# Building one-hot factors for tile 1's dense expert weights during tile 1's rows, in one layer of a streaming encoder

## The chip, the cores and the metric

One core of a Trainium2 chip runs the kernel. The metric is device time in microseconds (us); three runs of the kernel before took 1350.66, 1354.59 and 1364.85 us, median 1354.59.

## The reference

One layer of an encoder runs over 384 tokens of 1024 floats: 256 new tokens of one stream and 8 streams of 16. Attention in two branches comes first. The part that matters here is the feed-forward part, with 16384 experts of one neuron each:

```
def block(hx):                                   # 128 tokens
    q = (hx @ w_pq).reshape(128, 8, 256)         # 8 heads
    s1, s2 = q[..., :128] @ c1.T, q[..., 128:] @ c2.T
    v1, i1 = top_k(s1, 16);  v2, i2 = top_k(s2, 16)
    cand = v1[..., :, None] + v2[..., None, :]   # 256 pairs
    sv, si = top_k(cand, 16)
    e = (i1 * 128 + i2) at si                    # 16 experts a head
    g = softmax(sv)
    a = gelu(einsum('nhkd,nd->nhk', u[e], hx))
    return einsum('nhk,nhkd->nd', g * a, v[e])
```

So each token has 128 slots, each an expert with two keys (0 to 127) and a weight g * a. The tables u and v have 16384 rows of 1024 floats, 64 MB each.

## The kernel before

There are three tiles of 128 tokens: tiles 0 and 1 (lanes A and B, the new stream) and tile 2 (lane C, the 8 streams, `SAMPLE`). After the opening attention work of lane A, VectorE runs a loop over 512 "rows". Row n, for n below 384, is slot n % 128 of tile n // 128: GpSimd gathers for each of the 128 tokens its row of u into one of six slots of `rows_ring` (L699, 128 x 1024 floats, 512 KB), and VectorE takes the dot product with the token's `h2` (L1680). Rows 384 to 511 are tile 2's rows of v, also gathered, which VectorE multiplies by their weights and adds to `x1` (L1685).

Tiles 0 and 1 do not gather v. Their weights are spread into a dense matrix of token by expert, `dense[t]`, and at the end TensorE multiplies it with the whole of v (L1315): SyncE streams v in 128 blocks of 512 KB through four slots of `ring0`, and each block has two tiles times two halves of products (1024 matmul records in all). This product starts when all 64 groups are in `dense` and lane C's queries are done. The last addition to `x1` (L1696) follows both the product and row 511.

The dense weights are built in groups of four tokens, 32 groups a tile (`dense_weights`, on three engines). First the tile's keys 1, keys 2 and weights are turned (transposed) by TensorE into one PSUM bank (L1288) and copied to `turned` by ScalarE (L923, L924). Then, for each group:

- ScalarE builds the unweighted one-hot factor of key 2: for each token |iota - key2| (L962, four instructions), then relu(1 - that) over the four (L965), into one of two slots of `hot2`.
- VectorE builds the weighted factor of key 1: for each token (iota == key1) * weight (L1667, four instructions), into one of two slots of `hot1`.
- TensorE multiplies the two for each token (L1300, eight matmul records a group) into one of two PSUM banks (`transA`, `accumA`).
- ScalarE copies the bank to `dense` (L947), called "put" below.

The factors wait for the product two groups back, and the product for the put two groups back.

All work beside the rows is laid by step numbers: m is a quarter of the row number, and each engine takes up laid work in the order of its m. On VectorE and GpSimd, which carry the rows, laid work is taken up after every second row, that is at every half step. Tile 1's rows end at m = 64. `DENSE[t]` holds the step of the turning, that of the first group, and the groups per step; `dense_at` makes each group's step from it. Tile 1 has (64.5, 65, 4): turning at 64.5, groups from 65 on, two per pair of rows. The weights of tile 1 (gelu on ScalarE L914, times gate on VectorE L1655) are laid at m = 65 on VectorE. Each engine runs its own instructions strictly in this order, so an instruction that waits holds up all behind it.

Of the kernel before, what the change touches and what calls it, by code (L numbers as in the profile page):

```python
# [14 lines left out]
P = 128  # L15
# [103 lines left out]
def route_at(first, last=3):  # L119
# [25 lines left out]
def build(nc, i, o):  # L145

    with ExitStack() as ctx:  # L147
# [160 lines left out]
        built = [trans[0], accum[0]]  # L308

# [407 lines left out]
        def _(act):  # L717
# [198 lines left out]
            def dense_weights(t):  # L916
# [6 lines left out]
                act.activation(turned[:, 1, :], bank[:, 1, :], ACT.Copy, scale=-1.0).then_inc(S("turned_copied"), 1)  # L923
                act.activation(turned[:, 0::2, :], bank[:, 0::2, :], ACT.Copy).then_inc(S("turned_copied"), 1)  # L924
# [26 lines left out]
                for g in range(TGROUPS):  # L951
                    yield dense_at(t, g)
                    n = t * TGROUPS + g
                    if g == 0:
                        act.wait_ge(S("turned_copied"), 2 * t + 2)
                        act.wait_ge(S("iota_set"), 1)
                        if t == 0:
                            act.wait_ge(to(B, "logits_done"), 2)
                    if n >= 2:
                        act.wait_ge(S("built"), n - 1)  # L960
                    for j, tok in enumerate(tokens_of(t, g)):
                        act.activation(hot2[:, n % 2, j * P:j * P + P], iota[:, :], ACT.Abs,  # L962
                                       bias=turned[:, 1, tok:tok + 1]).then_inc(S("apart"), 1)
                    act.wait_ge(S("apart"), TOKENS * (n + 1))
                    act.activation(hot2[:, n % 2, :], hot2[:, n % 2, :], ACT.Relu, bias=1.0, scale=-1.0).then_inc(  # L965
                        S("hot2_ready"), 1)
                    if g:
                        put(g - 1)
                put(TGROUPS - 1)

            between = [laid(x) for x in (queries(A), softmax_exps(0), softmax_exps(1), groups(GL, LATE_COPY), steps(B),
                                         gate_copies(B), steps(C), gate_copies(C), queries(B), queries(C),
                                         softmax_exps(SAMPLE), gelus(0), dense_weights(0), gelus(1), dense_weights(1),
                                         late_scores(), gelus(SAMPLE))]
# [7 lines left out]
        def _(pe):  # L982
# [295 lines left out]
            def dense_weights(t):  # L1278
# [8 lines left out]
                for n, src in enumerate((keys[:, t, :, 0], keys[:, t, :, 1], dots[:, t, :])):  # L1287
                    ins = pe.transpose(built[0][:, n * P:n * P + P], src, ident[:, :])  # L1288
                ins.then_inc(S("turned"), 1)
                for g in range(TGROUPS):  # L1290
                    yield dense_at(t, g)
                    n = t * TGROUPS + g
                    pe.wait_ge(S("hot2_ready"), n + 1)
                    pe.wait_ge(S("hot1_ready"), n + 1)
                    if g == 1:
                        pe.wait_ge(S("turned_copied"), 2 * t + 2)
                    elif n >= 2:
                        pe.wait_ge(S("dense_put"), n - 1)
                    for j in range(TOKENS):
                        ins = pe.matmul(built[(g + 1) % 2][:, j * P:j * P + P], hot2[:, n % 2, j * P:j * P + P],  # L1300
                                        hot1[t][:, n % 2, j * P:j * P + P], start=True, stop=True)
                    ins.then_inc(S("built"), 1)

            between = [laid(x) for x in (queries(A), project(GL, LATE_PROJ), attention(B), gates(B), finish(B),
                                         attention(C), gates(C), finish(C), queries(B), dense_weights(0), queries(C),
                                         dense_weights(1))]
# [28 lines left out]
        def _(v):  # L1335
# [311 lines left out]
            def weights(t):  # L1647
# [3 lines left out]
                for q in range(parts):  # L1651
                    yield t * STEPS + STEPS // parts * (q + 1) + (2 if t == 0 else 1)
# [4 lines left out]
            def dense_weights(t):  # L1657

                for g in range(TGROUPS):
                    yield dense_at(t, g)  # L1660
                    n = t * TGROUPS + g
                    if g == 0:
                        v.wait_ge(S("turned_copied"), 2 * t + 2)
# [76 lines left out]
```

## Time and profile before

| | |
|---|---|
| median of three runs | 1354.59 us |
| profiled execution, device time | 1354.58 us |
| its span | 1352.8 us |
| TensorE busy | 1095.4 us (81%) |
| VectorE busy | 980.1 us (72%) |
| GpSimd busy | 657.9 us (49%) |
| ScalarE busy | 307.7 us (23%) |
| DMA moved | 460.64 MB, mean 341 GB/s |

The profile is of one execution. Its span is 1.8 us shorter than the device time of the same execution. The shares are averages over stages with different limits, so the rows further down are taken stage by stage: steps 48 to 64, the second build (tile 1's groups, 829 to 907 us), and the product (907 to 1347 us). Times in these rows are us from the start of the span; "idle before" is what an engine stood still just before an instruction, with the releaser behind the arrow.

### The profile page before, as it was taken

The numbers are of one execution on the slowest core, as the hardware profiler recorded it, in microseconds if no ns is written. First come the engines' busy times: TensorE is split into PE (matmuls) and PEld (weight loads), VectorE is DVE, ScalarE is ACT, GpSimd is POOL, SyncE is SP. The second block draws the span as 40 slices with busy tenths as digits, with TensorE's granted clock in tenths as the row PEclk, the third lists the DMA queues.
The fourth block names the chain that finished last, engine by engine and source line by source line (L and its number), as shares of the span: only waits on it lengthen the run. The fifth ranks groups of instructions, "written<-read, shape, count | busy, mean of one in ns | idle before, by whom it ended". The sixth has DMA issues, their size and how long they took to land. (4 is left out here: it accounts for less than half of the span.)

```text
span 1352.8 us, 13110 instructions
## 1 busy us (share of the span) xinstructions
PE 1095.4 (81%) x4321; PEld 732.2 (54%) x4321; DVE 980.1 (72%) x2230; ACT 307.7 (23%) x843; POOL 657.9 (49%) x570
## 2 busy tenths in 40 slices
PE   6888898886686768668566743779999999999998
PEld 3443583342243667325446732666666666666665
DVE  2621069999777799948988998999866566665666
ACT  2132122132311223031444454970000000000000
POOL 2110036557264565446674566566655454444452
PEclk9999899997797879786778865779999999999999
DMA  9985569969899999998997878779999999999998
GB/s 332 329 314 205 206 246 356 338 220 372 336 330 368 391 316 382 381 354 329 336 377 252 303 269 289 237 226 393 409 410 409 409 409 410 410 409 409 410 407 333
DMA packets 167348, 460.64 MB, mean 341 GB/s; under 512 B 14912, under 2 KB 36848, under 8 KB 167024
## 3 DMA queue, kind: packets, MB, share of 16 engines
q0 software_dynamic: 74784, 271.66, 53.7%
q1 hardware_dynamic: 92496, 188.14, 37.5%
q8 instruction: 34, 0.56, 0.2%
q14 instruction: 34, 0.28, 0.1%
HBM read 453.41 MB, written 6.34 MB: 340 GB/s over the span
## 5 line engine op out<-in xcount | busy, mean ns | idle before, releaser
L699 POOL DMA_INDIRECT rows_ring<-in_peer_u,expert x384 | 489.2, 1274 | 393.6 <-DVE dots L1680 293.8
L1680 DVE CUSTOM_DVE_ANT_0 rows_ring<-rows_ring,arena 128x1024 f32<-128x1024 f32 x384 | 458.3, 1223 | 93.1 <-DMA rows_ring<-in_peer_u,expert 89.9
L1315 PE MATMUL wide<-ring,arena 128*128 128x512 f32 x1024 | 440.2, 592 | 0.7 <-issue 0.7
L1315 PEld LDWEIGHTS wide<-ring,arena 128*128 128x128 f32 x1024 | 302.2, 295 | 138.1 <-issue 1.6
L1685 DVE SCALAR_TENSOR_TENSOR x<-rows_ring,dots,x 128x1024 f32<-128x1024 f32 x128 | 164.5, 1285 | 95.3 <-DMA rows_ring<-in_peer_v,expert 94.9
L699 POOL DMA_INDIRECT rows_ring<-in_peer_v,expert x128 | 125.0, 977 | 138.8 <-DVE x L1685 127.2
L962 ACT ACTIVATE hot<-iota,turned 128x128 f32<-128x128 f32 x256 | 81.0, 390 | 0.0
L993 PE MATMUL transB<-ident,arena 128*128 128x128 f32 x165 | 32.8, 329 | 40.3 <-ACT arena L732 15.9
L732 ACT ACTIVATE arena<-transB 128x512 f32<-128x512 f32 (+2 forms) x44 | 24.7, 564 | 126.1 <-PE transB L993 120.6
L993 PEld LDWEIGHTS transB<-ident,arena 128*128 128x128 f32 x165 | 22.1, 165 | 49.1 <-ACT arena L732 19.6
L1300 PE MATMUL accumA<-arena,hot 128*128 128x128 f32 x128 | 24.2, 348 | 29.9 <-ACT hot L965 16.1
L1018 PE MATMUL accumA<-ring,arena 128*128 128x512 f32 (+1 forms) x96 | 40.7, 582 | 7.8 <-DMA ring<-in_w_in 6.6
L1300 PE MATMUL transA<-arena,hot 128*128 128x128 f32 x128 | 25.7, 364 | 25.0 <-ACT hot L965 21.7
L1667 DVE TENSOR_SCALAR arena<-iota,turned 128x128 f32<-128x128 f32 x128 | 35.7, 360 | 8.5 <-PE transA L1300 5.9
L1265 PE MATMUL wide<-arena 128*128 128x128 f32 x320 | 40.8, 293 | 0.8 <-ACT arena L732 0.8
L1265 PEld LDWEIGHTS wide<-arena 128*128 128x128 f32 x320 | 40.3, 210 | 1.1 <-issue 1.1
L965 ACT ACTIVATE hot<-hot 128x512 f32<-128x512 f32 x64 | 40.3, 630 | 2.0
L614 POOL TENSOR_SCALAR ssx<-ssx 128x1 f32<-128x1 f32 x6 | 2.0, 339 | 79.1 <-ACT rows_ring L720 72.0
L1300 PEld LDWEIGHTS accumA<-arena,hot 128*128 128x128 f32 x128 | 21.1, 249 | 34.0 <-ACT hot L965 18.5
L1667 DVE TENSOR_SCALAR gain<-iota,turned 128x128 f32<-128x128 f32 x128 | 35.6, 362 | 5.1 <-PE accumA L1300 3.5
L1018 PE MATMUL accumA<-arena 128*128 128x512 f32 x80 | 35.3, 594 | 2.7 <-ACT accumA L763 1.9
L1300 PEld LDWEIGHTS transA<-arena,hot 128*128 128x128 f32 x128 | 22.1, 259 | 28.6 <-ACT hot L965 24.4
(300 smaller groups left out, 1397.2 us busy)
## 6 DMA issues: line engine op xcount, KB each, us to landing
ring<-in_peer_v SPq DMA_DIRECT2D x128, 512.0 KB, 6.8
arena<-in_w_in SPq DMA_DIRECT2D x15, 2048.0 KB, 16.3
ring<-in_w_in SPq DMA_DIRECT2D x9, 2048.0 KB, 17.2
arena<-in_w_pq SPq DMA_DIRECT2D x7, 2048.0 KB, 13.8
ring<-in_w_pq SPq DMA_DIRECT2D x5, 2048.0 KB, 17.8
arena<-in_w_out SPq DMA_DIRECT2D x4, 2048.0 KB, 10.9
arena<-in_w_br_a SPq DMA_DIRECT2D x3, 2048.0 KB, 10.2
ring<-in_w_br_b SPq DMA_DIRECT2D x3, 2048.0 KB, 12.0
```

Source lines behind the costliest of these rows:

```text
L699: pool.indirect_dma_start(rowbuf[:, n % ROWS, :], None, u_rows if n < U_ROWS else v_rows, index).then_inc(S(f"rows{n % ROWS}"), 16)
L732: ins = act.activation(dst, src, ACT.Copy)
L962: act.activation(hot2[:, n % 2, j * P:j * P + P], iota[:, :], ACT.Abs, bias=turned[:, 1, tok:tok + 1]).then_inc(S("apart"), 1)
L965: act.activation(hot2[:, n % 2, :], hot2[:, n % 2, :], ACT.Relu, bias=1.0, scale=-1.0).then_inc(S("hot2_ready"), 1)
L993: ins = pe.transpose(L.trans[n % count][:, m * P:m * P + P], src, ident[:, :])
L1018: ins = pe.matmul(accum[u % 2][:, 0:GROUPS[g][2]], L.hT[:, c, :], slot_weights(G.name, name)[:, c, :], start=c == 0, stop=c == DC - 1)
L1265: ins = pe.matmul(L.query_banks[k % 2][:, 0:P], slot_weights(L.name, f"pq{q}")[:, c, k * P:k * P + P], L.h2T[:, c, :], start=c == 0, stop= ...
L1300: ins = pe.matmul(built[(g + 1) % 2][:, j * P:j * P + P], hot2[:, n % 2, j * P:j * P + P], hot1[t][:, n % 2, j * P:j * P + P], start=True, ...
L1315: return pe.matmul(wide[:, 2 * t + half, :], dense[t][:, :, b], vblock[:, b % VBLOCKS, half * 512:half * 512 + 512], start=b == 0, stop=b ...
L1667: ins = v.tensor_scalar(hot1[t][:, n % 2, j * P:j * P + P], iota[:, :], turned[:, 0, tok:tok + 1], turned[:, 2, tok:tok + 1], ALU.is_equal ...
L1680: v.tensor_tensor_reduce(row, row, h2[:, t, :], 1.0, 0.0, ALU.mult, ALU.add, dots[:, t, k:k + 1]).then_inc(S("row_used"), 1)
L1685: v.scalar_tensor_tensor(out=x1[:, SAMPLE, :], in0=row, scalar=dots[:, SAMPLE, k:k + 1], in1=x1[:, SAMPLE, :], op0=ALU.mult, op1=ALU.add). ...
```

## The change

Tile 1's factors of key 2 need no weights, only keys, which are known well before the rows end. Seventeen of tile 1's 32 factors are now built by ScalarE between steps 48 and 64, into fifteen stretches of the arena that are part of `dense[1]` or free by then (`AHEAD`; the groups that those stretches belong to, `HELD`, are put last), and the two slots of `hot2`. The keys of tile 1 are turned by TensorE at step 47 into `sumB` and copied at 47.5 into the space of `own` and `new_bias`. The other fifteen factors are built during the second build, one after every second put, each in the place of a factor that was used. In the second build only the weights are turned. The second build is laid earlier and denser: turning at 64, groups from 64.5 at six per step, and the weights at 64 on VectorE.

```diff
-DENSE = [(35, 44, 1.8), (64.5, 65, 4)]
+DENSE = [(35, 44, 1.8), (64, 64.5, 6)]
+AHEAD = [22528, 23040, 23552, 24064, 16384, 16896, 25600, 30208, 18944, 19456, 19968, 20480, 20992, 21504, 22016]
+AHEAD_AT = [48, 49, 50, 51, 52, 53, 54, 55, 56, 57, 58, 61, 61.5, 62, 62.5, 63, 63.5]
+HELD = [(a - BLOCKS * P) // (TOKENS * P) for a in AHEAD]
-         list(range(TGROUPS))]
+         [n for n in range(TGROUPS) if n not in HELD] + HELD]
...
+        ahead = [part(a, TOKENS * P) for a in AHEAD] + [hot2[:, n, :] for n in range(2)]
+        key1_ahead, key2_ahead = new_bias[:, :, :].rearrange("p h k -> p (h k)"), own[:, :]
+        def hot2_of(t, g):
+            return ahead[g % len(ahead)] if t else hot2[:, g % 2, :]
...
# ScalarE, dense_weights
                 for g in range(TGROUPS):
                     yield dense_at(t, g)
+                    if t:
+                        if g:
+                            put(g - 1)
+                        late = len(ahead) + g // 2 - 1
+                        if g and g % 2 == 0 and late < TGROUPS:
+                            act.wait_ge(S("built"), TGROUPS + late - len(ahead) + 1)
+                            one_hots(1, late, key2_ahead)
+                        continue
...
+            def one_hots(t, g, keys2):
+                dst = hot2_of(t, g)
+                for j, tok in enumerate(tokens_of(t, g)):
+                    act.activation(dst[:, j * P:j * P + P], iota[:, :], ACT.Abs, bias=keys2[:, tok:tok + 1]).then_inc(
+                        S(f"apart{t}"), 1)
+                act.wait_ge(S(f"apart{t}"), TOKENS * (g + 1))
+                act.activation(dst, dst, ACT.Relu, bias=1.0, scale=-1.0).then_inc(S(f"hot2_ready{t}"), 1)
+            def one_hots_ahead():
+                yield AHEAD_AT[0] - 0.5
+                act.wait_ge(S("ahead_turned"), 1)
+                act.wait_ge(to(C, "logits_read"), 1)
+                act.activation(key2_ahead, sumB[:, P:2 * P], ACT.Copy, scale=-1.0).then_inc(S("ahead_copied"), 1)
+                act.activation(key1_ahead, sumB[:, 0:P], ACT.Copy).then_inc(S("ahead_copied"), 1)
+                for g in range(len(ahead)):
+                    yield AHEAD_AT[g]
+                    if g == 0:
...
+                    elif g == len(AHEAD):
+                        act.wait_ge(S("built"), TGROUPS)
+                    one_hots(1, g, key2_ahead)
...
# TensorE, dense_weights
-                    ins = pe.transpose(built[0][:, n * P:n * P + P], src, ident[:, :])
+                    if t == 0 or n == 2:
+                        ins = pe.transpose(built[0][:, n * P:n * P + P], src, ident[:, :])
...
+            def keys_ahead():
+                yield AHEAD_AT[0] - 1
+                pe.wait_ge(S("routed"), 8)
+                pe.wait_ge(to(C, "attended"), 2)
+                for n in range(2):
+                    ins = pe.transpose(sumB[:, n * P:n * P + P], keys[:, 1, :, n], ident[:, :])
+                ins.then_inc(S("ahead_turned"), 1)
...
# VectorE, weights and dense_weights
-                    yield t * STEPS + STEPS // parts * (q + 1) + (2 if t == 0 else 1)
+                    yield t * STEPS + STEPS // parts * (q + 1) + (2, 0, 1)[t]
...
+                    keys1 = key1_ahead if t else turned[:, 0, :]
```

VectorE, where the second build begins. The `ISA rows_ring,dots` rows are the dot products (the `ISA dots` rows between them only store their sums), `dots<-dots,gate` makes the weights, `gain<-iota` builds factors of key 1, four instructions a group. Before:

```order
L1680 ISA rows_ring,dots<-rows_ring,arena 128x1024
L1680 ISA dots 128x1
L1655 TENSOR_TENSOR dots<-dots,gate 128x128
L1667 TENSOR_SCALAR gain<-iota,turned 128x128 x4
L1680 ISA rows_ring,dots<-rows_ring,arena 128x1024
L1680 ISA dots 128x1
L1680 ISA rows_ring,dots<-rows_ring,arena 128x1024
L1680 ISA dots 128x1
L1667 TENSOR_SCALAR gain<-iota,turned 128x128 x8
```

Now (line numbers are those of the changed kernel):

```order
L1715 TENSOR_TENSOR dots<-dots,gate 128x128
L1743 ISA rows_ring,dots<-rows_ring,arena 128x1024
L1743 ISA dots 128x1
L1743 ISA rows_ring,dots<-rows_ring,arena 128x1024
L1743 ISA dots 128x1
L1730 TENSOR_SCALAR gain<-iota,new_bias,turned 128x128 x4
L1743 ISA rows_ring,dots<-rows_ring,arena 128x1024
L1743 ISA dots 128x1
L1743 ISA rows_ring,dots<-rows_ring,arena 128x1024
L1743 ISA dots 128x1
L1730 TENSOR_SCALAR gain<-iota,new_bias,turned 128x128 x12
```

The weights moved from behind row 261 to behind row 257, two rows now lie between them and the first group, and three groups instead of two follow each pair of rows; the 32nd group stands behind row 281 instead of row 293.

ScalarE, at the start of the second build, behind the gelu of tile 1 (`dots<-dots`); `hot<-` and, in the change, `arena<-iota,own` are factors of key 2, `arena<-accumA` and `arena<-transA` are puts. Before:

```order
L914 ACTIVATE dots<-dots 128x128
L923 ACTIVATE turned<-transA 128x128
L924 ACTIVATE turned<-transA 128x2x128
L897 ACTIVATE keys<-wide 128x512
L897 ACTIVATE tables<-wide 128x512
L962 ACTIVATE hot<-iota,turned 128x128 x4
L965 ACTIVATE hot<-hot 128x512
L962 ACTIVATE hot<-iota,turned 128x128 x4
L965 ACTIVATE hot<-hot 128x512
L947 ACTIVATE arena<-accumA 128x512
```

Now:

```order
L990 ACTIVATE hot<-iota,own 128x128 x4
L993 ACTIVATE hot<-hot 128x512
L925 ACT_TABLE_LOAD
L925 ACTIVATE dots<-dots 128x128
L935 ACTIVATE turned<-transA 128x128
L908 ACTIVATE keys<-wide 128x512
L908 ACTIVATE tables<-wide 128x512
L961 ACTIVATE arena<-accumA 128x512
L961 ACTIVATE arena<-transA 128x512
L990 ACTIVATE arena<-iota,own 128x128 x4
L993 ACTIVATE arena<-arena 128x512
L961 ACTIVATE arena<-accumA 128x512
```

A factor stood ahead of every put; now one stands behind every second put, and the last factors built ahead stand right ahead of the gelu.

ScalarE, near step 48, where the first factor is built ahead; `arena,ssx<-x` sums the squares for tile 2's row scale. Before:

```order
L947 ACTIVATE arena<-accumA 128x512
L962 ACTIVATE hot<-iota,turned 128x128 x4
L965 ACTIVATE hot<-hot 128x512
L947 ACTIVATE arena<-transA 128x512
L720 ACTIVATE arena,ssx<-x 128x1024
```

Now:

```order
L961 ACTIVATE arena<-accumA 128x512
L990 ACTIVATE arena<-iota,own 128x128 x4
L993 ACTIVATE arena<-arena 128x512
L990 ACTIVATE hot<-iota,turned 128x128 x4
L993 ACTIVATE hot<-hot 128x512
L961 ACTIVATE arena<-transA 128x512
L731 ACTIVATE arena,ssx<-x 128x1024
```

One whole factor now stands between the put and the group ahead of the squares.

## Rows read from the trace of the kernel before

**Rows 1.** Page, part 4: the chain that ended last, its share of the span by line.
```profile
PE wide L1315 33%; ACT hot L962 3%; ACT hot L965 1%; ACT arena L947 1%; PE accumA L1300 0%; DVE x L1696 0%; PE transA L1300 0%; PE transA L1288 0%; ACT keys L897 0%; DVEq L147 0%; ACT tables L897 0%; DVE dots L1655 0%; ACT dots L914 0%; ACT turned L924 0%; ACT turned L923 0%
```

**Rows 2.** Chain that ended last, pieces in order: start us, length us, what.
```profile
830.80 1.15 ACT hot L962 x4
831.97 0.64 ACT hot L965
...
904.36 1.74 PE transA L1300 x8
906.83 440.17 PE wide L1315 x1024
...
1347.07 0.69 DVE x L1696
```

**Rows 3.** Timeline, VectorE: start us, length us, line, operation xcount [idle before <-releaser]; in the second build.
```profile
855.12 1.22 DVE L1680 CUSTOM_DVE_ANT_0 rows_ring<-rows_ring,arena 128x1024 f32<-128x1024 f32 x1
856.26 2.14 DVE L1667 TENSOR_SCALAR gain<-iota,turned 128x128 f32<-128x128 f32 x8
858.32 1.22 DVE L1680 CUSTOM_DVE_ANT_0 rows_ring<-rows_ring,arena 128x1024 f32<-128x1024 f32 x1
```

**Rows 4.** Stretches: busy us (count) of PE, PEld, DVE, ACT, POOL; granted clock, DMA share, GB/s.
```profile
812.00:828.00 16.00, 0.00 (x0) 0.00 (x0) 11.90 (x21) 0.31 (x1) 12.65 (x12) 0.50 0.93 318
829.00:906.80 77.80, 53.89 (x258) 46.12 (x257) 73.39 (x198) 74.83 (x198) 44.34 (x34) 0.71 0.73 236
907.00:1340.00 433.00, 433.00 (x1009) 297.64 (x1010) 289.70 (x438) 6.02 (x9) 222.61 (x212) 1.00 1.02 406
```

**Rows 5.** Groups of VectorE, 906.83 to 1347.1: xcount | busy, mean ns | idle before, releaser.
```profile
L1685 DVE SCALAR_TENSOR_TENSOR x<-rows_ring,dots,x 128x1024 f32<-128x1024 f32 x128 | 164.5, 1285 | 95.3 <-DMA rows_ring<-in_peer_v,expert 94.9
L1680 DVE CUSTOM_DVE_ANT_0 rows_ring<-rows_ring,arena 128x1024 f32<-128x1024 f32 x88 | 106.6, 1225 | 47.2 <-DMA rows_ring<-in_peer_u,expert 46.8
```

**Rows 6.** Timeline, VectorE, 1338 to 1353: the last five rows of v.
```profile
1340.08 6.85 DVE L1685 SCALAR_TENSOR_TENSOR x<-rows_ring,dots,x 128x1024 f32<-128x1024 f32 x5 [0.80 <-DMA rows_ring<-in_peer_v,expert]
```

**Rows 7.** Timeline, VectorE: end of row 257, weights behind row 261, first group.
```profile
821.61 0.08 DVE L1680 DVE_READ_ACCUMULATOR2_ANT dots<- 128x1 f32 x1
...
827.95 0.28 DVE L1655 TENSOR_TENSOR dots<-dots,gate 128x128 f32<-128x128 f32 x1
829.91 0.34 DVE L1667 TENSOR_SCALAR gain<-iota,turned 128x128 f32<-128x128 f32 x1 [1.68 <-issue]
```

**Rows 8.** Timeline, VectorE: what follows the last group of the second build.
```profile
903.62 0.18 DVE L1655 TENSOR_TENSOR dots<-dots,gate 128x32 f32<-128x32 f32 x1
```

**Rows 9.** Timeline, TensorE: products of three groups, the first two in a row.
```profile
832.66 2.08 PE L1300 MATMUL accumA<-gain,hot 128*128 128x128 f32 x8 [3.43 <-ACT hot L965]
834.53 2.03 PE L1300 MATMUL transA<-gain,hot 128*128 128x128 f32 x8
...
855.73 1.16 PE L1300 MATMUL accumA<-gain,hot 128*128 128x128 f32 x8 [1.15 <-ACT hot L965]
```

**Rows 10.** Groups of ScalarE, 675.5 to 818: the costliest wait.
```profile
L880 ACT ACTIVATE arena<-wide 128x128 f32<-128x128 f32 x16 | 4.4, 277 | 36.0 <-PE wide L1265 36.0
```

**Rows 11.** Timelines of ScalarE, GpSimd and VectorE around the row scale of tile 2.
```profile
685.27 1.05 ACT L720 ACTIVATE arena<-x 128x1024 f32<-128x1024 f32 x1
686.50 0.29 POOL L614 TENSOR_SCALAR ssx<-ssx 128x1 f32<-128x1 f32 x1 [3.19 <-ACT arena L720]
689.80 1.23 DVE L1680 CUSTOM_DVE_ANT_0 rows_ring<-rows_ring,arena 128x1024 f32<-128x1024 f32 x1 [0.52 <-DMA rows_ring<-in_peer_u,expert]
```

**Rows 12.** Waits of VectorE, 675.5 to 819.2: total us, times, longest us.
```profile
DVE arena L1667 <- PE transA L1300: 5.7, 2, 5.1
```

**Rows 13.** Timeline, ScalarE, between the first build and the second.
```profile
809.08 0.60 ACT L947 ACTIVATE arena<-transA 128x512 f32<-128x512 f32 x1 [2.72 <-PE transA L1300]
809.70 1.28 ACT L914 ACT_TABLE_LOAD   x1
818.05 0.31 ACT L914 ACTIVATE dots<-dots 128x128 f32<-128x128 f32 x1 [7.06 <-DVE dots L1680]
```

More of the change, by code:

```diff
@@ L922, in dense_weights @@
                 bank = built[0][:, 0:3 * P].rearrange("p (a n) -> p a n", a=3)
-                act.activation(turned[:, 1, :], bank[:, 1, :], ACT.Copy, scale=-1.0).then_inc(S("turned_copied"), 1)
-                act.activation(turned[:, 0::2, :], bank[:, 0::2, :], ACT.Copy).then_inc(S("turned_copied"), 1)
+                if t:
+                    act.activation(turned[:, 2, :], bank[:, 2, :], ACT.Copy).then_inc(S("turned_copied"), 1)
+                else:
+                    act.activation(turned[:, 1, :], bank[:, 1, :], ACT.Copy, scale=-1.0).then_inc(S("turned_copied"), 1)
+                    act.activation(turned[:, 0::2, :], bank[:, 0::2, :], ACT.Copy).then_inc(S("turned_copied"), 1)
                 def put(g):
@@ L952, in dense_weights @@
                     yield dense_at(t, g)
-                    n = t * TGROUPS + g
+                    if t:
+                        if g:
[5 more added lines that the diff above has]
+                        continue
                     if g == 0:
-                        act.wait_ge(S("turned_copied"), 2 * t + 2)
+                        act.wait_ge(S("turned_copied"), 2)
                         act.wait_ge(S("iota_set"), 1)
[L957 to L966, printed above, removed]
+                        act.wait_ge(to(B, "logits_done"), 2)
+                    if g >= 2:
+                        act.wait_ge(S("built"), g - 1)
+                    one_hots(0, g, turned[:, 1, :])
                     if g:
@@ L975, in _ @@
+                                         dense_weights(1), late_scores(), gelus(SAMPLE))]
             start_laid(between)
@@ L1662, in dense_weights @@
                     if g == 0:
-                        v.wait_ge(S("turned_copied"), 2 * t + 2)
+                        v.wait_ge(S("turned_copied"), t + 2)
+                        if t:
+                            v.wait_ge(S("ahead_copied"), 2)
                     if n >= 2:
                         v.wait_ge(S("built"), n - 1)
+                    keys1 = key1_ahead if t else turned[:, 0, :]
                     for j, tok in enumerate(tokens_of(t, g)):
-                        ins = v.tensor_scalar(hot1[t][:, n % 2, j * P:j * P + P], iota[:, :], turned[:, 0, tok:tok + 1],
+                        ins = v.tensor_scalar(hot1[t][:, n % 2, j * P:j * P + P], iota[:, :], keys1[:, tok:tok + 1],
                                               turned[:, 2, tok:tok + 1], ALU.is_equal, ALU.mult)
```

25 lines of the change are left out of this document (18 added, 7 removed).

## The prediction

> **What bounds the kernel now.** I read the chain that ended last first. A third of the span is the product [rows 1]; it runs from 906.83 us without a break for 440.17 us, and the last sums start at 1347.07 [rows 2]. Ahead of it the chain runs through ScalarE: a factor of key 2 takes 1.15 + 0.63 us [rows 2], then comes a put, and so on for 32 groups. The stretches agree: in the second build ScalarE is busy 74.8 of 77.8 us [rows 4]. Read that way, a change that takes 17 factors of about 1.8 us off ScalarE starts the product some 30 us earlier.
>
> The same rows say more. In that stretch VectorE is busy 73.4 of 77.8 us [rows 4], so behind ScalarE there are only about 4 us before VectorE bounds. And in the product DMA is full: share 1.02, 406 GB/s over 433 us, against 236 GB/s in the second build [rows 4]. The product is TensorE's bound, but the gathered rows run beside it, and VectorE waits for them: 94.9 + 46.8 us [rows 5]. In the product 88 rows of u and 128 of v are used, 216 in all [rows 5], 2.04 us each. The last five start at 1340.08 and end at 1346.93 [rows 6], 0.14 us before the final sums. So two streams end together: TensorE's product, and the rows, which are paced by DMA. To end earlier both must.
>
> **The change, part by part.**
>
> *The start.* The weights stand behind row 257 instead of 261. Row 257 ended at 821.61; rows 258 to 261 took until 827.95, 6.3 us, and then VectorE stood 1.68 us until the turned weights were copied [rows 7]. Now two rows cover that wait.
>
> *VectorE's work from 821.61 to its last group.* A row takes 1.14 us and two groups 2.06 us [rows 3], so 1.03 us a group. There are now 24 rows (258 to 281) and 32 groups: 0.3 (weights, [rows 7]) + 24 x 1.14 + 32 x 1.03 = 60.6 us. The first four rows were short of DMA: 6.3 us where 4.6 would do; I keep 1.5 us of it (bounds 0 and 1.8).
>
> *Waits for TensorE.* VectorE now makes three groups in a row with two slots of `hot1`, so the third waits for the product of the first. A product takes 1.16 us at the granted clock 1.0 (2.4 GHz) and 2.08 us at 0.5 (1.2 GHz) [rows 9]. With 0.1 us for each signal (an estimate, from the gaps between such rows), the third may start 1.03 + 0.2 + 1.16 = 2.4 us after the first started, where VectorE would be ready at 2.06: 0.33 us lost in each of 10 such triples, 3.3 us in all. At 1.2 GHz it is 1.25 us, 12.5 us in all. The mean clock of this stretch was 0.71 [rows 4], more than half of it at the lower level; but TensorE gets the same work in less time, so I take the price nearer to the upper level: 5 us.
>
> *ScalarE in the second build* has 32 puts of 0.6 us and 15 factors of 1.8 us, 46 us; it no longer bounds.
>
> *The end of the build.* From VectorE's last group to the product it was 906.83 - 903.62 = 3.2 us [rows 2, 8]: product, put, start. That stays.
>
> *Upstream, steps 48 to 64.* ScalarE gets 17 x 1.8 = 31 us more and two small copies. It has room: 36 us there are waits for TensorE's queries alone [rows 10], and a factor that stands in such a wait costs nothing. Two places are not covered. One factor (step 48) stands ahead of the squares that give tile 2's row scale; GpSimd already waited 3.19 us for them with gathers queued behind, and VectorE then ran out of rows [rows 11]. And around step 50 TensorE and ScalarE wait for each other in turn while VectorE waits for them, 5.1 us at worst [rows 12]; a factor there lengthens it by up to 1.8 us. Two such delays are 3.6 us; all 17 on the path would be 31, none 0. I take 2.5 us. TensorE's two early turnings are taken from the second build, where they stood ahead of its first product. At the end of the stretch the last five factors (9 us) follow the last put at 809.08 + 0.5, then a table load of 1.28 and the gelu of 0.31 [rows 13]: about 820.3, just ahead of VectorE at 821.6. Nothing taken, but the cover is 1.3 us.
>
> *The product* then starts at 821.6 + 2.5 + 60.6 + 1.5 + 5 + 3.2 = 894.4, that is 12.4 us earlier, and ends at 894.4 + 440.2 = 1334.6.
>
> *The rows.* This is the price of the denser build: the last group stands behind row 281, not 293, so 12 rows more are left when the product starts. DMA is full all through the product, so these are not made up in it. When it ends 12 rows are left, with VectorE's pace of 6.85 / 5 = 1.37 us a row [rows 6]; 512 KB at 406 GB/s [rows 4] would be 1.29. I take 1.37: 16.4 us. The last row ends at 1351.0 instead of 1346.9.
>
> *Sum.* 1351.0 + 0.1, and from the first sum to the end of the span 1352.8 - 1347.1 = 5.7: span 1356.8. With the 1.8 us around the span: 1358.6 us, against 1354.58 of the same execution, which is also the median of the runs. So 4 us or 0.3% slower: the start gained 12.4, the rows lost 16.4. The break-even is a build that lets the product start at 890.3.
>
> **A rule of the skill against the row.** While the product ran DMA moved 406 GB/s [rows 4]. The Trainium skill (DMA: Bandwidth & Descriptors, Specifications) gives 435 GB/s as the fabric's ceiling and about 358 GB/s as a core's share of HBM. The trace lies above the second and 7% below the first, so the measured figure is the one to use; by 435 GB/s the 12 rows would cost 14.5 us, an estimate from that page.
>
> On TensorE the row shows both clock levels within one build, with products between short waits for ScalarE [rows 9]. The Trainium skill (TensorE: Matmul & The Clock Gate, HAM oscillation) says that micro-idles between groups let the clock fall again. The trace agrees so far, since both levels occur; by that rule the denser build, with its pauses behind each triple, could stay low, which would be the third rival below.
>
> **The rivals.**
>
> *The rows come along* (faster). If the product alone set the end, it would be 1334.6 + 5.7 + 1.8 = 1342.1 us; with no upstream delay and TensorE at 2.4 GHz, 1338. For it: TensorE is the engine on the chain, without a gap. Against it: VectorE's 141.7 us of waits for gathered rows in the same stretch, and DMA at its limit there. It would need 12 rows, 6.3 MB, more in 440 us than ever passed. 10% for an end nearer to this than to mine, and of it about half below -1%.
>
> *A smooth build* (no change or a little less). TensorE at 2.4 GHz (3.3 us) and no delay upstream: product at 890.2, end 1354.4. 22%.
>
> *TensorE stays at 1.2 GHz* (slower). Then the waits cost 12.5 instead of 5 us: 1366 us. For it: 0.71 now, and the stretch ahead of the build was all at 0.50, with TensorE idle [rows 4]. Against it: more products in less time. 12%.
>
> *ScalarE's factors land on the path upstream* (slower). If more than two of the uncovered ones hit TensorE's chain or the gelu comes late, each adds 1.8 us; from seven on (9 us above my sum) it is 1% slower, 1368 and above. Against it: the 36 us of waits. 8%.
>
> **How the numbers follow.** My sum has 48%. The first rival reaches down to 1338, the last two up to 1370; leaving out half of the first and part of the last, the range is 1345 to 1368. About 1% is what a measurement of this kernel can tell from no change. Faster by over 1% (below 1341): half of the first rival and little else, 6%. Slower by over 1% (above 1368): most of the last rival and a corner of the third, 9%. Within 1%: 85%.
>
> **What would show it.** Right: the product starts near 894 and the chain's last part is no longer TensorE but the rows (L1685 or its DMA), 10 to 14 rows after the last product; DMA stays near 406 GB/s while it runs; VectorE, not ScalarE, is the full engine in the second build, with waits for TensorE of 3 to 12 us. Wrong: the product ends last, with rows done before it (then DMA had room); or the product starts after 900 (clock, or upstream delay: row 257 ends later than 824).

## The result and the profile after

The changed kernel took 1369.24 us (median of 12 runs, 1361.28 to 1373.69) against 1354.06 us of the kernel before (12 runs, 1346.86 to 1364.85). The ratio of the runs is 1.0098, 95% interval 1.0073 to 1.0124: 13 us slower, between 10 and 17 (the two medians lie 15 us apart). The forecast was 4 us slower, with a range of 1345 to 1368. On the forecast's base of 1354.58 us the ratio gives 1367.9, at the upper edge of the range; the raw median lies 1.2 us above it. The ratio is just within the 1% that the forecast called no change, and its interval reaches past that. The profiled execution of after took 1364.52 us, span 1362.7, so 9.9 us more than the span of before. Executions of one kernel differ by some 0.7% either way here, so one profile can't carry a difference of a few us on absolute times. I read stretches that start at an event of the kernel instead. The start of row 192 is the first one ahead of all that the change touches: it came at 673.1 us in after and at 675.5 in before. From there to the last row it is 683.8 us in after and 671.5 in before. That is 12.3 us, close to the 13 of the ratio. One run of a kernel further down (e4) took 3650.89 us, and no ratio uses it.

The chain that ended last, by engine and by line (page, part 4), where [rows 1] had 33% in the product:

```profile
DMA 33%; DVE 25%; PE 22%; ACT 6%; POOL 6%; issue 6%; SPq 0%; DVEq 0%; ACTq 0%; POOLq 0%
DMA rows_ring<-in_peer_v,expert 15%; DMA rows_ring<-in_peer_u,expert 13%; DVE rows_ring L1743 9%; POOL rows_ring L710 6%; DMA ring<-in_w_in 4%; PE wide L1315 3%; DVE x L1748 2%; PE accumB L1089 2%; PE accumA L1089 2%; PE accumB L1068 2%; ACT hot L990 1%; PE accumA L1351 1%; PE transA L1351 1%; PE accumA L1291 1%; PE accumA L1315 1%
```

The product (now L1375) is no longer in it. The rows are, with the DMA that brings them. The stretches of after, columns as in [rows 4] (second build, product, and the 15 us that follow):

```profile
829.00:896.00 67.00, 43.43 (x250) 40.33 (x251) 60.51 (x175) 43.82 (x106) 30.90 (x24) 0.80 0.60 190
...
900.00:1335.00 435.00, 435.00 (x1010) 298.04 (x1010) 290.12 (x451) 6.51 (x10) 228.17 (x213) 1.00 1.02 406
1335.00:1350.00 15.00, 5.57 (x13) 3.36 (x12) 13.26 (x12) 0.00 (x0) 11.88 (x10) 0.79 0.93 328
```

ScalarE fell from 74.8 of 77.8 us to 43.8 of 67, VectorE has 60.5 of 67: it is the busiest engine there, but not a full one. DMA moved 190 GB/s in the build where it moved 236. In the product it is full, at 406 GB/s as before. TensorE from the end of the build on:

```profile
892.71 1.23 PE L1351 MATMUL accumA<-gain,arena 128*128 128x128 f32 x8
895.79 1.42 PE L1351 MATMUL transA<-gain,arena 128*128 128x128 f32 x8 [1.85 <-ACT arena L993]
897.94 14.49 PE L1375 MATMUL wide<-ring,arena 128*128 128x512 f32 x27 [0.73 <-issue]
```

VectorE at the end (rows of v on L1748, final sums on L1759); the product ended at 1340.5:

```profile
1333.82 12.39 DVE L1748 SCALAR_TENSOR_TENSOR x<-rows_ring,dots,x 128x1024 f32<-128x1024 f32 x9 [0.65 <-DMA rows_ring<-in_peer_v,expert]
1346.66 1.28 DVE L1748 SCALAR_TENSOR_TENSOR x<-rows_ring,dots,x 128x1024 f32<-128x1024 f32 x1 [0.45 <-DMA rows_ring<-in_peer_v,expert]
1348.30 5.45 DVE L1748 SCALAR_TENSOR_TENSOR x<-rows_ring,dots,x 128x1024 f32<-128x1024 f32 x4 [0.35 <-DMA rows_ring<-in_peer_v,expert]
1354.20 2.67 DVE L1748 SCALAR_TENSOR_TENSOR x<-rows_ring,dots,x 128x1024 f32<-128x1024 f32 x2 [0.46 <-DVE x L1748]
1357.02 2.48 DVE L1759 TENSOR_TENSOR x<-wide,x 128x512 f32<-128x512 f32 x4
```

Twelve rows end after the product, the last at 1356.9: 16.3 us in which TensorE is done and the kernel is not. In before none did [rows 6]. Beside the product VectorE still waits for the gathered rows as in [rows 5]:

```profile
L1748 DVE SCALAR_TENSOR_TENSOR x<-rows_ring,dots,x 128x1024 f32<-128x1024 f32 x117 | 150.3, 1284 | 86.9 <-DMA rows_ring<-in_peer_v,expert 86.5
L1743 DVE CUSTOM_DVE_ANT_0 rows_ring<-rows_ring,arena 128x1024 f32<-128x1024 f32 x101 | 122.2, 1225 | 57.1 <-DMA rows_ring<-in_peer_u,expert 56.7
```

### The profile page after: what moved, and what is told of

The parts are those of the page before. It is cut to its first block, busy times and chain, and to the rows that moved or that the text cites. A ratio compares the mean times of both kernels' runs of the same rounds, so it can differ in the third digit from the quotient of the medians.

```text
span 1362.7 us, 13115 instructions
## 1 busy us (share of the span) xinstructions
PE 1091.6 (80%) x4321; PEld 729.7 (54%) x4321; DVE 982.3 (72%) x2230; ACT 309.7 (23%) x844; POOL 662.9 (49%) x570
## 4 chain that ended last, share of the span: by engine, by line
DMA 33%; DVE 25%; PE 22%; ACT 6%; POOL 6%; issue 6%; SPq 0%; DVEq 0%; ACTq 0%; POOLq 0%
DMA rows_ring<-in_peer_v,expert 15%; DMA rows_ring<-in_peer_u,expert 13%; DVE rows_ring L1743 9%; POOL rows_ring L710 6%; DMA ring<-in_w_in 4%; PE wide L1315 3%; DVE x L1748 2%; PE accumB L1089 2%; PE accumA L1089 2%; PE accumB L1068 2%; ACT hot L990 1%; PE accumA L1351 1%; PE transA L1351 1%; PE accumA L1291 1%; PE accumA L1315 1%
## 5 line engine op out<-in xcount | busy, mean ns | idle before, releaser
L1375 PE MATMUL wide<-ring,arena 128*128 128x512 f32 x1024 | 442.6, 595 | 0.7 <-issue 0.7
L1375 PEld LDWEIGHTS wide<-ring,arena 128*128 128x128 f32 x1024 | 302.5, 296 | 140.5 <-issue 4.9
L1748 DVE SCALAR_TENSOR_TENSOR x<-rows_ring,dots,x 128x1024 f32<-128x1024 f32 x128 | 164.4, 1284 | 89.0 <-DMA rows_ring<-in_peer_v,expert 87.3
L1351 PE MATMUL accumA<-arena,hot 128*128 128x128 f32 x128 | 27.4, 381 | 35.4 <-ACT hot L993 22.0
L990 ACT ACTIVATE hot<-iota,turned 128x128 f32<-128x128 f32 x128 | 40.5, 389 | 0.0
L1730 DVE TENSOR_SCALAR gain<-iota,new_bias,turned 128x128 f32<-128x128 f32 x128 | 35.7, 358 | 6.5 <-PE transA L1351 3.2
L1043 PE MATMUL transA<-ident,arena 128*128 128x128 f32 x94 | 17.9, 315 | 25.8 <-DVE arena L1402 8.1
L990 ACT ACTIVATE arena<-iota,own 128x128 f32<-128x128 f32 x120 | 38.0, 390 | 0.0
```

The costliest lines, as they stand in the source:

```text
L990: act.activation(dst[:, j * P:j * P + P], iota[:, :], ACT.Abs, bias=keys2[:, tok:tok + 1]).then_inc(S(f"apart{t}"), 1)
L1043: ins = pe.transpose(L.trans[n % count][:, m * P:m * P + P], src, ident[:, :])
L1375: return pe.matmul(wide[:, 2 * t + half, :], dense[t][:, :, b], vblock[:, b % VBLOCKS, half * 512:half * 512 + 512], start=b == 0, stop=b ...
L1730: ins = v.tensor_scalar(hot1[t][:, n % 2, j * P:j * P + P], iota[:, :], keys1[:, tok:tok + 1], turned[:, 2, tok:tok + 1], ALU.is_equal, AL ...
L1748: v.scalar_tensor_tensor(out=x1[:, SAMPLE, :], in0=row, scalar=dots[:, SAMPLE, k:k + 1], in1=x1[:, SAMPLE, :], op0=ALU.mult, op1=ALU.add). ...
```

## The experiments

One table for all, from the profiles (us). "Upstream" is the start of row 192 to the end of row 257. "Build" is from there to the end of VectorE's last group, "gap" from that to the product. "Row stream" is the end of row 257 to the end of the last row. "Rows left" end after the product. "Whole" is from the start of row 192 to the end of the product or of the last row, whichever is later. The ratio is that of the run times to before's, with its 95% interval.

| kernel | upstream | build | gap | product | row stream | rows left | whole | ratio |
|---|---|---|---|---|---|---|---|---|
| before | 146.2 | 82.0 | 3.1 | 440.2 | 525.2 | 0 | 671.5 | 1 |
| after | 152.5 | 70.1 | 2.2 | 442.6 | 531.3 | 12 | 683.8 | 1.0098 [1.0073, 1.0124] |
| e1_rate4 | 155.5 | 72.4 | 1.9 | 441.8 | 518.8 | 2 | 674.3 | 1.0004 [0.9971, 1.0037] |
| e2_dense6_alone | 147.5 | 75.5 | 4.1 | 441.7 | 536.1 | 11 | 683.6 | 1.0101 [1.0056, 1.0146] |
| e3_ahead_alone | 152.4 | 76.2 | 1.9 | 441.5 | 519.7 | 1 | 672.1 | 1.0014 [0.9981, 1.0047] |
| e4_after_less12 | 151.8 | 71.1 | 2.5 | 442.4 | 514.9 | 0 | 667.8 | 0.9937 [0.9909, 0.9966] |
| e5_before_less12 | 147.3 | 81.4 | 3.6 | 442.1 | 504.2 | 0 | 674.4 | 0.9973 [0.9941, 1.0006] |
| e6_eight_rate4 | 147.6 | 73.8 | 8.7 | 441.7 | 522.9 | 0 | 671.9 | 0.9990 [0.9959, 1.0021] |
| e7_eight_rate6 | 147.3 | 70.9 | 8.8 | 441.7 | 533.7 | 9 | 681.0 | 1.0058 [1.0030, 1.0086] |
| e8_eight_lead | 146.5 | 72.1 | 1.9 | 443.3 | 518.0 | 1 | 664.5 | 0.9948 [0.9911, 0.9986] |
| e9_six_at_48 | 150.7 | 73.5 | 8.8 | 441.8 | 521.7 | 0 | 674.8 | 0.9973 [0.9943, 1.0003] |
| e10_six_at_53 | 149.1 | 72.3 | 8.8 | 441.7 | 518.5 | 0 | 671.8 | 0.9990 [0.9956, 1.0023] |

The column "whole" is of one execution each, and the ratio of six to twelve, so they agree only to a few us: in e9 they lie 7 us apart, in e5 6.6. e8, e9 and e10 ran on another chip than e1 to e7; each ratio is to runs of before on the same chip.

**The two halves of the change apart.** The theory: the rows that are left cost the time, and they come from the six groups per step. The rival: the seventeen factors on ScalarE upstream cost it. e1 keeps the factors and takes the old rate; e3 keeps them and takes the old laying as a whole; e2 is the new laying without the factors.

```
e1, against after:   -DENSE = [(35, 44, 1.8), (64, 64.5, 6)]
                     +DENSE = [(35, 44, 1.8), (64, 64.5, 4)]
e2, against before:  -DENSE = [(35, 44, 1.8), (64.5, 65, 4)]
                     +DENSE = [(35, 44, 1.8), (64, 64.5, 6)]
                     -  ... + (2 if t == 0 else 1)      # the weights' step
                     +  ... + (2, 0, 1)[t]
e3, against after:   -DENSE = [(35, 44, 1.8), (64, 64.5, 6)]
                     +DENSE = [(35, 44, 1.8), (64.5, 65, 4)]
                     -  ... + (2, 0, 1)[t]
                     +  ... + (2, 1, 1)[t]
```

> The change with four groups per step in the second build instead of six, all else kept. In the change the product started at 897.9 us, ended at 1340.6, and the last row ended 16.3 us after it. Theory R (the rows left behind by the denser build set the end): the last group stands behind row 291 instead of 281, so the product starts some 5 us later, near 903, and only about 2 rows are left when it ends, so the span is 8 to 10 us shorter than that of the change, near that of the kernel before. Rival S (the start of the product sets the end): 5 us longer than the change.

> The kernel before with only the laying of the second build changed as in the change (turning and weights at 64, groups from 64.5 at six per step); no factor is built ahead. Theory R: ScalarE still needs 2.3 us a group, so the product starts some 4 to 6 us earlier than before, near 902, but 12 rows are left when it ends, so the run is 8 to 12 us longer than before. Rival S: 4 to 6 us shorter than before.

> The change with the second build laid as before (turning at 64.5, groups from 65 at four per step, weights at 65); the factors are still built ahead. Theory R with a delay upstream of 4 to 6 us by the factors built ahead: row 257 ends 4 to 6 us later than before, the build itself is about 4 us shorter than before since VectorE instead of ScalarE paces it, no row is left behind, and the time is within 3 us of before. If there is no delay upstream, 4 us shorter than before. Rival S without a delay: the same 4 us shorter.

Measured: the laying alone (e2) is 1.0101, as much as the whole change costs, and a little more than the 8 to 12 us that were expected. The factors with the old rate (e1) or the old laying (e3) are 1.0004 and 1.0014, neither to be told from no change. Rows left: 11 with the dense laying, 2 and 1 without. The second build of e3, of e2 and of e1, in that order:

```profile
827.00:902.00 75.00, 46.08 (x249) 40.92 (x249) 73.73 (x198) 44.35 (x109) 46.35 (x37) 0.73 0.79 265
```

```profile
824.00:899.00 75.00, 51.82 (x245) 44.39 (x246) 61.97 (x177) 71.80 (x189) 33.20 (x26) 0.69 0.58 185
```

```profile
833.00:905.00 72.00, 47.56 (x249) 42.43 (x249) 71.74 (x198) 44.59 (x110) 46.09 (x36) 0.72 0.80 261
```

In the same 75 us DMA moved 265 GB/s with four groups per step and 185 with six: 6.0 MB less, which is 11 rows of 512 KB. e3 and e2 differ in the factors, too; e1 and after differ in the rate alone, and there it is 261 against 190 GB/s, some 5 MB or 10 rows in 72 us, with 2 against 12 rows left. The dense laying gives VectorE's slots to groups, so ring slots come free later and GpSimd starts fewer gathers (26 operations on it instead of 37). What isn't moved here is left when the product ends, since DMA is full until then. The end of e2, where the product ended at 1345.6:

```profile
1339.09 13.79 DVE L1685 SCALAR_TENSOR_TENSOR x<-rows_ring,dots,x 128x1024 f32<-128x1024 f32 x10 [0.47 <-DMA rows_ring<-in_peer_v,expert]
1353.16 4.06 DVE L1685 SCALAR_TENSOR_TENSOR x<-rows_ring,dots,x 128x1024 f32<-128x1024 f32 x3 [0.28 <-DMA rows_ring<-in_peer_v,expert]
1357.67 2.67 DVE L1685 SCALAR_TENSOR_TENSOR x<-rows_ring,dots,x 128x1024 f32<-128x1024 f32 x2 [0.46 <-DVE x L1685]
```

**Twelve rows off, in after and in before.** If the rows set the end of after and the product that of before, taking rows 500 to 511 off shortens the first and not the second.

```
-            for n in range(U_ROWS + SLOTS):
+            for n in range(U_ROWS + SLOTS - 12):       # GpSimd's and VectorE's loops
...
-            v.wait_ge(S("row_used"), U_ROWS + SLOTS)
+            v.wait_ge(S("row_used"), U_ROWS + SLOTS - 12)
```

> The change without the last 12 rows of v of tile 2 (rows 500 to 511 are neither gathered nor added, so twelve slots of each token of tile 2 are left out of its output). Theory R: the last row then ends about when the product does, and the span is 14 to 17 us shorter than that of the change. Rival S (the product sets the end): no difference.

> The kernel before without the last 12 rows of v of tile 2 (rows 500 to 511 are left out, as in e4). In the kernel before both streams end together. Theory R: the product still ends where it did, so the span is 0 to 2 us shorter than before, not 16. If the rows alone set the end before, too: 14 to 17 us shorter.

Measured: after falls from 1.0098 to 0.9937. That is 1.6%, 22 us give or take 5 by the ratios and 16 us by the column "whole", where 14 to 17 were expected. Before falls from 1 to 0.9973, with 1 in the interval. VectorE's last row and the sums, of e4 and then of e5:

```profile
1338.03 5.45 DVE L1748 SCALAR_TENSOR_TENSOR x<-rows_ring,dots,x 128x1024 f32<-128x1024 f32 x4 [0.47 <-DMA rows_ring<-in_peer_v,expert]
1343.62 2.48 DVE L1759 TENSOR_TENSOR x<-wide,x 128x512 f32<-128x512 f32 x4
```

```profile
1327.02 1.28 DVE L1685 SCALAR_TENSOR_TENSOR x<-rows_ring,dots,x 128x1024 f32<-128x1024 f32 x1 [0.90 <-DMA rows_ring<-in_peer_v,expert]
1346.01 0.69 DVE L1696 TENSOR_TENSOR x<-wide,x 128x512 f32<-128x512 f32 x1 [17.71 <-PE wide L1315]
```

In e5 VectorE stands 17.71 us for the product: the rows had been done. In e4 the rows end 1.2 us ahead of the product. So the change moved the end from the product to the rows. The 0.9937 also shows about what the earlier product start is worth once the rows don't cover it: 8.5 us (5 to 12) against before, and 5 us against e5, which leaves out the same rows; the intervals of e4 and e5 overlap, so these 5 us are not clear of noise.

**Fewer factors ahead.** The next question: ScalarE was the chain's engine in the build, and VectorE was only 4 us behind it, so a few factors less on ScalarE would do. Here eight are built ahead, at steps 58 to 63, six in the arena and two in the slots of `hot2`; in the build three factors follow four puts. e6 has four groups per step, e7 six.

```
-DENSE = [(35, 44, 1.8), (64, 64.5, 6)]
+DENSE = [(35, 44, 1.8), (64, 64.5, 4)]                 # e6 only
...
+AHEAD = [22528, 23040, 23552, 24064, 16384, 16896]
+AHEAD_AT = [58, 59, 60, 61, 61.5, 62, 62.5, 63]
...
-                        late = len(ahead) + g // 2 - 1
-                        if g and g % 2 == 0 and late < TGROUPS:
+                        late = len(ahead) + g - g // 4 - 1
+                        if g % 4 and late < TGROUPS:
```

> Only eight factors are built ahead, at steps 58 to 63, in six stretches of the arena and the two slots; in the second build, which is laid as in the change but with four groups per step, three factors follow every four puts. Theory R with the upstream delay due to the factors at steps 48 to 57 (U): row 257 ends within 2 us of before, the product starts near 899 and ends near 1341 with about 2 rows left, and the time is 4 to 7 us shorter than before. If the delay has another cause (the run, or any factor wherever it stands): row 257 ends 4 us later than before, and the time is that of before.

> As e6, eight factors ahead at steps 58 to 63, but with six groups per step as in the change. Theory R with U: row 257 ends within 2 us of before, the product starts near 893, 12 rows are left when it ends, and the time is 3 to 6 us longer than before, 4 to 6 us shorter than the change. Without U: the time of the change. Rival S: 13 us shorter than before.

Measured: e6 0.9990, e7 1.0058. The rate alone is 0.7% with eight factors and 0.9% with seventeen (e1 against after). Upstream fell from 152.5 to 147.6 and 147.3. But e6 gained nothing over before, where 4 to 7 us were expected, and e7 lost 8 us instead of 3 to 6. In the trace both have a gap of some 8.8 us between VectorE's last group and the product, where before had 3.1. TensorE's last groups in e6:

```profile
891.50 2.08 PE L1344 MATMUL transA<-gain,arena 128*128 128x128 f32 x8 [2.51 <-ACT arena L993]
896.09 2.08 PE L1344 MATMUL accumA<-gain,hot 128*128 128x128 f32 x8 [2.51 <-ACT hot L993]
900.68 2.08 PE L1344 MATMUL transA<-gain,hot 128*128 128x128 f32 x8 [2.51 <-ACT hot L993]
903.49 2.91 PE L1368 MATMUL wide<-ring,arena 128*128 128x512 f32 x3 [0.73 <-issue]
```

The lead of eight shrinks by one with every fourth group and is used up by the end. Then each factor waits for the product that frees its place, each product for that factor, 4.6 us a group, and the products run at 2.08 us, as at the lower clock level in [rows 9]; the granted clock from 889 to 903 us was 0.50.

**The lead kept.** The same as e6, with five factors per six puts, so the lead lasts.

```
-                        late = len(ahead) + g - g // 4 - 1
-                        if g % 4 and late < TGROUPS:
+                        late = len(ahead) + g - g // 6 - 1
+                        if g % 6 and late < TGROUPS:
```

> As e6 (eight factors ahead at steps 58 to 63, four groups per step), but in the second build five factors follow every six puts instead of three every four, so that the factors stay two or more groups ahead up to the end. In e6 the lead shrinks to none and the last groups take 4.6 us each, with the product 8.7 us behind VectorE's last group instead of 2 to 3. Theory: the product then starts 5 to 6 us earlier than in e6, near 897; if the rows and not the product set the end by then, the span is only 1 to 3 us shorter than in e6, some 4 to 6 us shorter than before. Rival S: 5 to 6 us shorter than e6.

Measured: 0.9948, 0.9911 to 0.9986. Of the kernels that leave nothing out it is the only one whose whole interval lies below before: 7 us faster (2 to 12), where 4 to 6 were expected. The gap is 1.9 us again. Against e6 by itself the gain is 0.4%, which is not clear of the noise of the two ratios; the trace shows what became of the gap, not what the gap alone cost. The TensorE of e8, and its second build:

```profile
880.95 1.13 PE L1344 MATMUL transA<-gain,arena 128*128 128x128 f32 x8 [2.09 <-DVE gain L1723]
882.07 1.13 PE L1344 MATMUL accumA<-gain,hot 128*128 128x128 f32 x8
885.29 1.13 PE L1344 MATMUL transA<-gain,hot 128*128 128x128 f32 x8 [2.09 <-issue]
887.15 3.76 PE L1368 MATMUL wide<-ring,arena 128*128 128x512 f32 x4 [0.73 <-issue]
```

```profile
812.00:886.00 74.00, 46.59 (x255) 41.47 (x256) 73.97 (x200) 60.53 (x155) 46.80 (x37) 0.75 0.80 264
```

VectorE is busy 73.97 of 74.00 us. DMA moved 264 GB/s, against 236 in before, where VectorE stood for ScalarE. From the end of row 257 the product starts 11.0 us earlier than in before and the row stream ends 7.2 us earlier: both streams moved, and one row is left behind the product. This profiled execution was the fastest of twelve (1338.72 to 1357.47 us) and ahead of before's by 9 us at row 192 already, so its span of 1336.9 is not what e8 gains; the whole from row 192, 7.0 us shorter, and the ratio are.

**Where the delay upstream comes from.** Six of the eight factors at steps 48 to 53 (e9) or at 53 to 58 (e10), all else as e6.

```
-AHEAD_AT = [58, 59, 60, 61, 61.5, 62, 62.5, 63]
+AHEAD_AT = [48, 49, 50, 51, 52, 53, 62.5, 63]          # e9
+AHEAD_AT = [53, 54, 55, 56, 57, 58, 62.5, 63]          # e10
```

> As e6, but six of the eight factors stand at steps 48 to 53 (two at 62.5 and 63). From the start of row 192 to the end of row 257 the kernel before took 146.2 us, e2, e5, e6 and e7 147.3 to 147.6, and the four with 17 factors ahead 151.8 to 155.5. If factors ahead of the row scale and between TensorE's queries cause it (U): 149 to 152 us. If only many factors do: 147 to 148.

> As e9, but the six stand at steps 53 to 58. In the change VectorE waited 2.35 and 1.42 us at steps 56 and 57 where the kernel before waited 0.5 and nothing. If those waits come from the factors at steps 54 to 56: 149 to 151 us from row 192 to the end of row 257. If all of the delay comes from steps 48 to 52, as the prediction had it: 147 to 148.

Measured: upstream is 150.7 and 149.1, against 147.6 of e6. Without factors ahead of step 58 it was between 146.2 and 147.6 in six executions, with seventeen between 151.8 and 155.5 in four. That is 3 us more for the first place and 1.5 for the second, of one execution each, and the stretch differed by 1.4 us within the six and by 3.7 within the four. VectorE's waits for TensorE's products in the same stretch tell it more clearly: 7.7 to 8.2 us in the six, 10.3 in e9, 9.9 in e10, 12.0 to 15.5 in the four. So factors at either place lengthen these waits by some 2 us. The times, 0.9973 and 0.9990 against 0.9990 of e6, do not show it; what the delay is worth in the end is within the noise here. e8 against e1, both with four groups per step and no lost lead, are 0.9948 and 1.0004, which points the same way; but the two differ in more than the place and number of the factors, in the rate of late factors and in the chip.

## Why the prediction was right in its mechanism and short in its size

**Which stream sets the end: right.** "When it ends 12 rows are left": 12 were, and they took 16.3 us where 16.4 was put. e2, e4 and e5 show the cause from three sides. The rival of rows that come along is out: DMA moved 406 GB/s before and after in the product, and 217 rows ended in it instead of 216, at 2.04 us each as before. Of the other signs that were named, the product started at 897.9 us, near 894 and before 900; VectorE was not full in the build; and row 257 ended at 825.6, past the 824 that was named as the sign of a delay upstream.

**Upstream, 2.5 us: too small.** Row 192 to row 257 takes 152.5 instead of 146.2 us, 6.2 more. VectorE's waits in that stretch, of after and then of before, which answer to [rows 12]:

```profile
DVE rows_ring L1743 <- DMA rows_ring<-in_peer_u,expert: 7.1, 8, 1.5
DVE arena L1730 <- PE accumA L1351: 6.4, 4, 4.1
DVE arena L1730 <- PE transA L1351: 5.9, 2, 3.5
...
```

```profile
DVE arena L1667 <- PE transA L1300: 5.7, 2, 5.1
DVE rows_ring L1680 <- DMA rows_ring<-in_peer_u,expert: 5.5, 7, 1.2
DVE arena L1667 <- PE accumA L1300: 2.1, 2, 1.9
...
```

For TensorE's products of tile 0 they are 12.3 us where before had 7.8, and TensorE in turn waited there longer for ScalarE's factors of tile 0, 38.9 us (after) instead of 33.5 (before):

```profile
PE accumA L1351 <- ACT hot L993: 21.8, 10, 3.4
PE transA L1351 <- ACT hot L993: 17.1, 11, 2.4
...
```

```profile
PE transA L1300 <- ACT hot L965: 17.6, 9, 4.9
PE accumA L1300 <- ACT hot L965: 15.9, 9, 2.5
...
```

A factor ahead stands right in front of one of these, as at 698.27:

```profile
698.27 1.26 ACT L990 ACTIVATE arena<-iota,own 128x128 f32<-128x128 f32 x4
699.56 0.63 ACT L993 ACTIVATE arena<-arena 128x512 f32<-128x512 f32 x1
700.10 1.26 ACT L990 ACTIVATE hot<-iota,turned 128x128 f32<-128x128 f32 x4
```

So the 6.2 us are all in VectorE's waits: 4.5 more for these products, 1.6 more for rows, 0.2 in one other wait. The step that failed is the choice of the two places. At the squares GpSimd's wait did rise, from 3.19 [rows 11] to 5.22 us, but VectorE's waits for the rows behind it only from 3.0 to 3.1. In the place around the wait of 5.1 us [rows 12], VectorE stood 7.7 us instead of 7.0. The larger part, 4.4 us instead of 0.5, came later, at steps 56.5 to 59, while the first build of tile 0 still ran factor by factor. The two longest of these, and then the only one of before:

```profile
757.10 1.12 DVE L1730 TENSOR_SCALAR arena<-iota,turned 128x128 f32<-128x128 f32 x4 [2.35 <-PE transA L1351]
761.93 1.12 DVE L1730 TENSOR_SCALAR arena<-iota,turned 128x128 f32<-128x128 f32 x4 [1.42 <-PE accumA L1351]
```

```profile
756.37 1.11 DVE L1667 TENSOR_SCALAR arena<-iota,turned 128x128 f32<-128x128 f32 x4 [0.51 <-PE transA L1300]
```

In e9, which has factors at steps 48 to 53 and none from 54 to 62, VectorE stood 2.34 us at step 56.5, and 0.53 in e6, so factors that are laid earlier lengthen this wait, too. The 1.6 us for rows are within what the executions without factors ahead of step 58 show (5.5 to 7.0 us). And the 36 us of waits that the prediction took for cover [rows 10] covered little: after the change ScalarE still stood 29.6 of them, though 31 us of factors had been added.

```profile
L891 ACT ACTIVATE arena<-wide 128x128 f32<-128x128 f32 x16 | 4.4, 278 | 29.6 <-PE wide L1315 29.6
```

**The build, 67.1 us with its waits: 70.1.** The term that was too small is the wait of VectorE's third group for the product of the first. It was put at 5 us for ten triples, between 0.33 us each at the upper clock level and 1.25 at the lower. Both prices are in the trace. Two groups without a wait take 2.06 us [rows 3]; here the third group starts 2.38 us behind the first in one triple, 3.29 in the next:

```profile
862.65 2.23 DVE L1730 TENSOR_SCALAR gain<-iota,new_bias,turned 128x128 f32<-128x128 f32 x8
865.03 1.11 DVE L1730 TENSOR_SCALAR gain<-iota,new_bias,turned 128x128 f32<-128x128 f32 x4 [0.15 <-PE accumA L1351]
...
868.35 2.14 DVE L1730 TENSOR_SCALAR gain<-iota,new_bias,turned 128x128 f32<-128x128 f32 x8
871.64 1.11 DVE L1730 TENSOR_SCALAR gain<-iota,new_bias,turned 128x128 f32<-128x128 f32 x4 [1.16 <-PE transA L1351]
```

Four triples lost 0.32 us each, four lost 1.22 to 1.24 and two 1.0: 8.2 us in all, 3.2 more than was put. Rows short of DMA were put at 1.5 us and are 1.1 between the end of row 257 and the last group:

```profile
DVE rows_ring L1743 <- DMA rows_ring<-in_peer_u,expert: 1.1, 2, 0.6
```

So the rival of TensorE staying at 1.2 GHz came in part, for six triples of ten, though the mean clock of the build was 0.80. TensorE's products at the head of two triples, with the same wait ahead of them:

```profile
846.11 1.13 PE L1351 MATMUL transA<-gain,arena 128*128 128x128 f32 x8 [2.19 <-ACT arena L993]
...
869.56 2.04 PE L1351 MATMUL transA<-gain,arena 128*128 128x128 f32 x8 [2.19 <-ACT arena L993]
```

The Trainium skill (TensorE: Matmul & The Clock Gate, A second HAM failure mode: psum-queue depth-cycling) reports a kernel in which short idle times between groups of products let the clock swing between its two levels. This trace agrees: behind 2.19 us of idle time the products take 1.13 us in one triple and 2.04 in another, and the granted clock was 0.98 from 838 to 850 us and 0.72 from 868 to 874. In e6 the last products, each behind 2.51 us of waiting, all take 2.08 us.

**The end of the build, 3.2: 2.2.** At the other end of the build the gelu's cover held: it ended at 823.2 us, and the weights were taken up at 825.48, behind the late row 257.

**The product, 440.2: 442.6.** This does not look like an effect of the change: e5, with the build of before, has 442.1, and all the other kernels lie between 441.5 and 443.3. The kernel before was the shortest of twelve, and the prediction took one execution's value as fixed.

**The sum.** From row 192 on, the terms are off by 3.7 (upstream), 3.0 (build), -0.9 (gap), 2.4 (product) and -0.1 (rows left): 8.1 us, and with the forecast 4.1 that gives 12.2 of the 12.3 us by which the whole is longer. Put into the forecast's sum they make 1366.7 us, inside its range; the median of the runs is 2.5 us more. The rows' end is also to be had without the product: from row 257 the row stream takes 6.1 us more than before, with DMA at 190 GB/s in the build instead of 236, and 6.2 us were lost ahead of it.

**What the laying cost was not only the lost gain.** The prediction weighed 12.4 us of earlier start against 16.4 us of rows as if both came from the same cause. e1 and e8 separate them: with four groups per step most of the earlier start is kept (builds of 72.4 and 72.1 us, against 70.1 in after and 82.0 in before), and the rows are quicker as well, with VectorE busy nearly all the time where before it stood for ScalarE. e3, laid as before, keeps half of it (76.2). So the loss against before came with the six groups per step. Building ahead had a price, too: with seventeen factors the delay upstream took back what the build gained (e1, 1.0004), with eight late ones it did not (e8, 0.9948), as far as one kernel of each tells.

## What to carry to other kernels

Where two streams end together, count what is left of each when the last stretch begins: a denser laying that starts one earlier with the other's slots only moves the end to the other. Take the bounding engine's load away just as far as the next engine allows (eight factors were enough here, not seventeen), keep the share of the stream that is bound by DMA, and keep a lead that lasts to the end of the loop. An engine's idle time covers added work only where it lies at the instant at which the work comes up; a sum of idle times over 150 us does not show that it does.

## What the runs showed of the hardware

One core moved 401 to 406 GB/s over 410 to 443 us of gathers of 512 KB and streamed blocks together, in the product of all twelve kernels. The Trainium skill (DMA: Bandwidth & Descriptors, Specifications) gives about 358 GB/s as a core's share of HBM and 435 as the fabric's ceiling; the trace lies between. The 12 rows that were left went by neither figure, nor by the measured one, which would make 15.5 us: they took 16.3, and nine rows around the product's end ran on VectorE without a break in 12.39 us, some 1.38 each, so the prediction was right to take VectorE's pace of 1.37 [rows 6].

What I had not expected is the spread of the same program: the product's 1024 records took 440.2 to 443.3 us in twelve executions, and row 192 started between 666.6 and 677.6 us, although next to nothing differs ahead of it. The run times of one kernel vary by some 0.7% either way. A term of 2 us can't be read from the absolute times of two profiles.
